# Second expert stage: ring slots by rows of the weights, a size for 32 tokens, loops for large sizes, and nested size tests

## The reference

```python
def moe_ffn(h, router_w, router_b, w1, b1, w2, b2):        # xt: 256 x 1024
    logits = (xt @ router_w + router_b)
    top_v, top_e = lax.top_k(logits, 4)
    gate = jax.nn.softmax(top_v, axis=-1)
    ...
        hb = xb @ w1[e] + b1[e]                            # xb: the tokens of expert e
        g, u = hb[:, :1024], hb[:, 1024:]
        g = jnp.minimum(g, 7.0)
        u = jnp.clip(u, -7.0, 7.0)
        glu = g * jax.nn.sigmoid(g * 1.702)
        return ((u + 1.0) * glu) @ w2[e] + b2[e]           # times its gate, added to the token
```

## Time and profile before

| | us |
|---|---|
| median of 3 runs | 2518.3 (2500.11 to 2536.43) |
| profiled execution | 2512.87 |
| its span, first to last instruction | 2511.1 |
| busy: PE, its weight loads, DVE, ACT | 2247.6, 1328.1, 589.5, 370.2 |
| mean granted clock of PE | 0.916 |
| read from HBM | 616.55 MB |

### The profile page before, as it was taken

How to read it: one execution, slowest core, us unless ns; L and a number is a source line. 1 busy time by engine, 2 the same in 40 slices (tenths; PEclk the granted TensorE clock), 3 DMA queues, 4 the chain that set the end, 5 groups by cost and what they waited for, 6 DMA issues and landing times.

```text
span 2511.1 us, 32392 instructions
## 1 busy us (share of the span) xinstructions
PE 2247.6 (90%) x12228; PEld 1328.1 (53%) x12229; DVE 589.5 (23%) x1216; ACT 370.2 (15%) x718; POOL 6.5 (0%) x23
## 2 busy tenths in 40 slices
PE   7969877889998997788858999899999999999996
PEld 5655445556545686633335554445455555555553
DVE  2352512211222015500031212111221222222113
ACT  1032101121111014300011111101011111111111
POOL 1000000000000000000000000000000000000000
PEclk9989997999999976588877989999998999999998
DMA  8822253998966340022225999859799999999990
GB/s 289 317 101 82 86 201 120 327 356 312 325 224 233 102 150 19 1 100 100 100 78 198 393 363 345 312 202 380 270 386 381 339 393 376 393 383 393 384 370 18
DMA packets 272763, 621.67 MB, mean 248 GB/s; under 512 B 12200, under 2 KB 19026, under 8 KB 272510
## 3 DMA queue, kind: packets, MB, share of 16 engines
q1 hardware_dynamic: 272302, 616.95, 67.1%
q10 hardware_dynamic: 208, 0.67, 0.1%
HBM read 616.55 MB, written 1.05 MB: 246 GB/s over the span
## 4 chain that ended last, share of the span: by engine, by line
PE 87%; DVE 6%; issue 4%; ACT 3%; POOL 0%; ACTq 0%; DVEq 0%; POOLq 0%
PE pair L1616 26%; PE pair L1410 16%; PE pair L1652 10%; PE pair L1671 8%; PE pair L1397 6%; PE pair L1689 4%; PE pair L1621 3%; PE pair L1655 2%; PE pair L1459 2%; PE pair L1451 1%; PE pair L1825 1%; PE pair L1434 1%; PE pair L1422 1%; PE pair L1702 1%; PE pair L1414 1%
## 5 line engine op out<-in xcount | busy, mean ns | idle before, releaser
L1616 PE MATMUL pair<-ring,r_at 128*64 128x256 f32 (+1 forms) x4864 | 662.0, 402 | 53.2 <-issue 49.5
L1616 PEld LDWEIGHTS pair<-ring,r_at 128*64 128x64 f32 (+1 forms) x4864 | 385.6, 143 | 317.2 <-issue 177.2
L1652 PE MATMUL pair<-ring,r_big 128*64 128x512 f32 x1152 | 263.9, 609 | 0.0
L1410 PE MATMUL pair<-ring,x_T 128*128 128x512 f32 (+1 forms) x608 | 236.9, 545 | 2.5 <-ACT r_big L719 1.1
L1671 PE MATMUL pair<-r_big,r_mix 128*128 128x64 f32 (+1 forms) x1600 | 204.3, 290 | 23.1 <-DVE r_big L1338 11.4
L1671 PEld LDWEIGHTS pair<-r_big,r_mix 128*128 128x128 f32 x1600 | 197.8, 205 | 34.0 <-issue 33.2
L1173 DVE TENSOR_SCALAR r_big<-iota,rank 128x128 f32<-128x128 f32 x100 | 24.1, 283 | 752.0 <-PE pair L1621 577.0
L1410 PEld LDWEIGHTS pair<-ring,x_T 128*128 128x128 f32 x608 | 107.5, 190 | 125.0 <-issue 123.0
L1652 PEld LDWEIGHTS pair<-ring,r_big 128*64 128x64 f32 x1152 | 80.4, 140 | 151.2 <-issue 149.9
L1397 PE MATMUL pair<-x_T,ring 128*128 128x256 f32 x656 | 152.8, 391 | 7.8 <-DVEq L838 6.4
L1397 PEld LDWEIGHTS pair<-x_T,ring 128*128 128x128 f32 x656 | 125.9, 195 | 32.3 <-issue 8.0
(11 more groups left out here) (310 smaller groups left out, 1602.7 us busy)
## 6 DMA issues: line engine op xcount, KB each, us to landing
ring<-exp_w SPq DMA_DIRECT2D x192, 2048.0 KB, 12.5
ring<-w_in SPq DMA_DIRECT2D x24, 2048.0 KB, 9.2
ring<-w_gate SPq DMA_DIRECT2D x16, 2048.0 KB, 11.4
ring<-w_up SPq DMA_DIRECT2D x16, 2048.0 KB, 13.4
ring<-w_down SPq DMA_DIRECT2D x16, 2048.0 KB, 9.2
ring<-mod_w SPq DMA_DIRECT2D x12, 2048.0 KB, 13.5
ring<-w_out SPq DMA_DIRECT2D x4, 2048.0 KB, 8.0
ring<-w_branch SPq DMA_DIRECT2D x3, 2048.0 KB, 7.6
```

The costliest lines, as they stand in the source:

```text
L1410: ins = mm(out[:, t, 0:n], xT[:, k, P * t:P * t + P], w[:, k, c0:c0 + n], start=(k == 0), stop=(k == nk - 1 and bias is None))
L1616: ins = mm(out, stat(k), w_[:, k, c0:c0 + n], start=(k == 0), stop=(bias is None and k == KD - 1))
L1652: ins = mm(ps[2][H2 * h:H2 * h + H2, 0:512], hT[:, at:at + H2], cols, start=beg, stop=end)
```

## The change

The gate and up weights of an expert are loaded in four slots of 256 whole rows (2048 columns) in place of four of 1024 rows x 512 columns. The six slots stay. Sizes become four: up to 32, 64, 128, and more. The tests are nested, `If` and `Else`, the smallest size first, once for all of an expert's up slots and once for its down slots, with the slots' waits inside. For up to 32 tokens the stationary operand has 32 columns, and gate and up, two halves each, go to four column groups; for up to 64, two column groups. Up to 128: loops on PE (`nc.Fori`) over the four column blocks for slots 1 to 3, each slot closed by a drain. More than 128: loops over everything, both halves of the tokens at once. The picks repeat every 32 or 64 slots (`slots_of`), so that gather and scatter are always 128 wide and have no size test. The hidden layer is limited, multiplied and transposed in one piece instead of two halves. The wait for `outputs_added` leaves `add_outputs` for its callers. Item `kvc` ahead of the stage is split in two, which aligns the stage's first slot with the ring.

```diff
 def size_of(eng, e):
-    return eng.value_load(sizes[0:1, bass.ds(e + 1, 1)], min_val=0, max_val=2)
+    return eng.value_load(sizes[0:1, bass.ds(e + 1, 1)], min_val=0, max_val=3)
+def smallest_first(eng, size, body):
+    with eng.If(size == 0):
+        body(H4)
+    with eng.Else():
+        with eng.If(size == 1):
+            body(H2)
+        with eng.Else():
+            with eng.If(size == 2):
+                body(P)
+            with eng.Else():
+                body(T)
...
-def expert2(slot, kind, e, half, wait):
+def expert2(slot, part, e, wait):
     sp.wait_ge(PD, wait)
-    if kind < 2:
-        src = w1e[bass.ds(e * D, D), 1024 * kind + 512 * half:1024 * kind + 512 * half + 512]
-        nk = KD
+    if part < 4:
+        src, nk = w1e[bass.ds(e * D + 2 * P * part, 2 * P), :], 2
     else:
-        src = w2e[bass.ds(e * D + 512 * half, 512), :]
-        nk = 4
+        src, nk = w2e[bass.ds(e * D + 512 * (part - 4), 512), :], 4
...
 # ACT, per expert
-    for half in range(2):
-        act.wait_ge(sem("gate_limited"), 2 * e + (1 + half))
...
-        s.activation(SG[:, 0:4 * w], GS[:, 0:4 * w], ACT.Sigmoid, scale=1.702)\
-    turned(2, 0, e, w)
-    by_size(act, size_next, rows_of(2, e + 1))
-    turned(2, 1, e, w)
+        act.wait_ge(sem("gate_limited"), e + 1)
+        ins = s.activation(SG[0:rows, 0:n], GS[0:rows, 0:n], ACT.Sigmoid, scale=1.702)
+    ins.then_inc(sem("sig_ready"), 1)
+    rows_of(2, e + 1)(P)
+    hidden_T2(e, w)
     outputs_and_picks(2, e, w, 6 * e + (base_pd2 + 6))
...
 # DVE, per expert
+    slots = iota if b == 1 else slots_of[:, bass.ds(size_of(dve, e) * P, P)]
...
+    dve.wait_ge(PD, 6 * e + (base_pd2 + 4))
+    v.tensor_scalar(gate, g_in, 7.0, None, ALU.min).then_inc(sem("gate_limited"), 1)
+    ins = v.tensor_scalar(up, u_in, 7.0, -7.0, ALU.min, ALU.max)
+    ins.then_inc(up_free, 1)
+    v.scalar_tensor_tensor(out=up, in0=up, scalar=1.0, in1=gate, op0=ALU.add, op1=ALU.mult)\
+    v.tensor_tensor(out=out, in0=up, in1=sig, op=ALU.mult).then_inc(sem("hidden_ready2"), 1)
...
 # PE
+def up_parts(w):
+    x32, x64, x128 = [lambda k, n=n: XG[:, k, 0:n] for n in (H4, H2, P)]
+    if w == H4:
+        return [(ps[0][H4 * q:H4 * q + H4, 0:512], x32, q, H4) for q in range(4)]
...
+def up_slot(w, j, n, i, e, buf):
+    pe.wait_ge(slot_loaded[(j + n) % RING], value_of(j + n, i, 6))
...
+    if w == P and n == 0:
+        pe.wait_ge(sem("pickT_ready2"), e + 1)
+    if w == P and n:
+        pe.sem_inc(sem("wide_rows_begun"), 1)
+        with nc.Fori(0, 4, engines=[pe.engine]) as q:
+            for k in range(2 * n, 2 * n + 2):
+                mm(pairs[:, bass.ds(q * 512, 512)], XG[:, k],
+                   ring[:, bass.ds(q * 512 + (j + n) % RING * SLOT + 2048 * (k % 2), 512)],
+                   start=(k == 0), stop=False)
+        if n < 3:
+            ins = pe.drain()
+    else:
+        for k in range(2 * n, 2 * n + 2):
+            for out, stat, q, rows in up_parts(w):
+                ins = mm(out, stat(k), w_[:, k % 2, 512 * q:512 * q + 512], start=(k == 0), stop=False)
+    if n == 3:
+        for out, stat, q, rows in up_parts(w):
+            ins = mm(out, ones[32 * q:32 * q + 1, 0:rows], b1q[32 * q:32 * q + 1, buf], start=False, stop=True)
+    ins.then_inc(PD, 1)
...
+def down(j, i, size, e):
+    def body(w):
+        turn_hidden2(w, e)
+        pe.wait_ge(sem("outputs_added2"), e + 2)
+        pe.wait_ge(sem("hiddenT_ready2"), e + 1)
+        for half in range(2):
+            down_slot(w, j, half, i)
+    smallest_first(pe, size, body)
...
+def expert2(i, par, j, e, size):
+    pe.wait_ge(sem(f"b1_loaded{buf}"), 16 * (PASS // 2) * i + 16 * (par // 2) + 16)
+    pe.wait_ge(sem("xg_ready2"), e + 1)
+    up(j, i, size, e, buf)
+    scatter2(e)
+    gather2(e + 1, 1 - buf)
+    pe.wait_ge(sem("hidden_ready2"), e + 1)
+    down(j + 4, i, size, e)
+    pe.wait_ge(sem("xg_ready2"), e + 2)
+    turn_picks2(buf)
```

More of the change, by code:

```diff
@@ new lines, in outputs_of_all @@
+            def outputs_of_all(e):
+                dve.wait_ge(PD, 6 * e + (base_pd2 + 6))
+                for t in range(NT):
+                    for h in range(2):
+                        v.scalar_tensor_tensor(out=ACC[:, t, 512 * h:512 * h + 512], in0=ps[2 + t][:, 512 * h:512 * h + 512],
+                                               scalar=comb0[:, t, bass.ds(e + 1, 1)],
+                                               in1=ACC[:, t, 512 * h:512 * h + 512], op0=ALU.mult, op1=ALU.add)
+                v.memset(YS, 0.0).then_inc(sem("ys_ready2"), 1)
@@ L1613, in body @@
                                  for t in range(NT)]
                     for k in range(KD):
-                        for out, stat, c0, n, rows in parts:
-                            ins = mm(out, stat(k), w_[:, k, c0:c0 + n], start=(k == 0),
-                                     stop=(bias is None and k == KD - 1))
-                    if bias is not None:
-                        q, buf = bias
-                        for out, stat, c0, n, rows in parts:
-                            ins = mm(out, ones[32 * q:32 * q + 1, 0:rows], b1q[32 * q:32 * q + 1, buf, c0:c0 + n],
-                                     start=False, stop=True)
+                        for out, stat, c0, n in parts:
+                            ins = mm(out, stat(k), w_[:, k, c0:c0 + n], start=(k == 0), stop=(k == KD - 1))
@@ L1637, in turn_hidden, with half_down @@
                 by_size(pe, size, body)
-            def half_down(j, load_value, hT, size, first, last):
+            def half_down(j, load_value, size):
                 pe.wait_ge(slot_loaded[j % RING], load_value)
@@ L1645, in body @@
                     for f in range(4):
-                        beg, end = first and f == 0, last and f == 3
+                        beg, end = f == 0, f == 3
                         for h in range(2):
@@ new lines, in down_of_all @@
+            def down_of_all():
+                with nc.Fori(0, 2, engines=[pe.engine]) as o_:
+                    for c in range(KD):
+                        for t in range(NT):
+                            mm(pairs[:, bass.ds(o_ * 512 + 2048 + 1024 * t, 512)],
+                               HTF[:, 1024 * t + P * c:1024 * t + P * c + P], W2_all[:, bass.ds(o_ * 512 + D * c, 512)],
+                               start=(c == 0), stop=(c == KD - 1))
+                pe.drain().then_inc(PD, 2)
```

337 lines of the change are left out of this document (216 added, 121 removed).

## The result

The changed kernel takes 2487.8 us, the median of 8 runs (2478.8 to 2492.9), beside 2516.5 for the kernel before in the same comparison: a ratio of 0.9889, with a 95% interval of 0.985 to 0.9928. It is 1.1% faster, where 2.8% was forecast. The second expert stage takes 1118.5 us (1344.4 to 2462.9) where it took 1145.5, 27 less; the sum had 1062 for it, 83.5 less (70 with the 13 set aside for the clock).

What follows compares the result with a forecast made beforehand. PE bound the kernel, with the weight DMA close behind in the second expert stage. That stage was to fall from 1145.5 to 1062 us (-83); 2511 - 83 + 13 for the clock = 2441 span, 2448 us forecast, range 2395 to 2540.

Steps and rivals of the forecast that it cites:

- the 13 set aside for the clock: Second expert stage: 13 us added because PE's products run at a lower clock after waiting for weight slots.
- Up of size 0: Up products of experts with at most 32 tokens: four column groups at once, 115 ns a record, 8.5 us instead of 16.7.
- Rival 3: Groups of 32 columns don't run four at once; experts up to 32 tokens take 33.9 us: +182, 2630 us; chance 0.05.
- A size-0 expert on PE: PE's time for one expert of at most 32 tokens in the second stage: 22.2 us, against 30.6 before.
- The new wait for the hidden layer's copy: Before the down products, PE waits for ACT's copy of the turned hidden layer: 0.7 to 1.0 us.
- The loops: PE loops in wide experts, three slots of four turns: 0.3 us a slot taken.
- Rival 1: Loops in the four wide experts cost 1 to 3 us a turn: 2448 plus 48 to 144 us; chance 0.12.
- Rows of 8 KB: Up-weight transfers in whole rows: 417 GB/s instead of 385, so 30.4 us of DMA an expert instead of 32.1.
- rival 4: Longer up-weight rows bring nothing: 32.1 us for 30.4 over about 19 DMA-paced experts, +34, 2482 us; chance 0.13.
- rival 2: Long skips over unused size bodies miss, two per expert at 4.28 us plus slow clock: +200, 2648 us; chance 0.12.
- nearest is the skip, so nothing: PE's size tests: skipping about 78 products was priced at nothing, like today's skip of 27; bounds nothing and 4.28 us.
- less half an expert for a full ring at the start: Experts 17 to 30: the six-slot weight ring, full at the start, saves about half an expert, 410 us for 426.

Runs made afterwards that it cites:

- without the large body: The changed kernel without the body for more than 128 tokens in all size tests of the second stage: 2436.0 us, ratio 0.9688.
- padded version with short jumps: The changed kernel with size tests once per slot, large sizes tested first, and 128 never-run instructions ahead of the expert loop: 2436.8 us, ratio 0.9696.
- versions with 58 and 52 us of issue waits in all: The changed kernel with tests per slot and large sizes first (2442.3 us, 0.9726), and the changed kernel without the over-128-token body (2436.0 us, 0.9688).

## Why the prediction was wrong

The sign and most terms were right, the size was not: the profiled span came to 2486.7, against 2441 by the sum, 45.7 more. By stretches the measured times are over the forecast by 10.5, 24.8, 22.5 and -1.3; less the 13 set aside for the clock that is 43.5. The rest is a stage that began 3.8 us later (1344.4; in the runs that change only PE's code or the rows it began anywhere from 1332 to 1352, so that this is an effect of the change is not shown), an end 1.2 us shorter, and rounding.

**What held.**
- Up of size 0: 110 ns a record (115 taken, 107 to 222 the bounds); bias 1.06 (1.3); down 3.64 (3.7); scatter 3.70 where nothing was waited for; gather 3.7. Rival 3 falls.
- A size-0 expert on PE: 20.8 us, start to start, for the first one without the large body, which waits for nothing but the copy (22.2 by the sum). Wide experts 6, 8 and 11 took 61.6 to 61.8 (63.4), the 64-token experts of 5 to 16 31.4 to 34.2 in the padded version with short jumps (33.9).
- The new wait for the hidden layer's copy: 34.0 us in 28 experts, 1.2 each (0.7 to 1.0 taken).
- The loops: 0.7 us a slot at most, 5.3 us in all (0.3 a slot taken). Rival 1 falls.
- The wait for both clamps in wide experts: 11.4 us in four, 2.8 each, as worked out.
- Rows of 8 KB: over 400 GB/s, 415 in several slices of the page's row (417 forecast), and 20 us when they are taken away, where rival 4 had priced 34. Rival 4 falls.
- The 32-token size: 2.6%, about 66 us. By the sum's own numbers, 22 x (33.9 - 30.4) = 77.

Slips in the arithmetic are small: the parts listed for the three sizes add up to 22.0, 33.6 and 63.2, not 22.2, 33.9 and 63.4, some 3 us over experts 5 to 16. In rival 2's full price, "5 x 22" has no source in the text: two skips at 4.28 lift a size-0 expert by 8.6, not by 22.

**The step that failed** is "nearest is the skip, so nothing", the price of the size tests. The row it leaned on was a jump over 27 products; the change made it 78, and the bounds were 0 and 4.28. What the runs showed: a jump in a bad place costs 3.1 to 4.2 us behind the up body and 2.4 to 3.7 behind the down body. Over the stage, back edges and loops included, it is 160.6 us of issue waits. That this was coming, the prediction's own sign said: gaps put down to issue ahead of scatter and picks of size 0 were to show rival 2. The sum had held 6 x 7 = 42 for back edges and 4 for the loops. Of the 115 left, most of what fell in experts 17 to 30 lay in time in which PE would have waited for weights; what fell in experts 0 to 16 made them 623.3 for the 588 forecast, 35 us. The versions with 58 and 52 us of issue waits in all, near the 46 of the sum, took 582 and 583 there, so the rest of that sum was good to about 1%.

The waits were rival 2's mechanism, and its gauge was fair: "it decides from about 2 us a skip". The 115 us over two skips in 32 experts are 1.8 us a skip. I gave it a chance only at its full price, 2648, and left out its mild form, between the forecast and the threshold, which is what came. The Trainium skill (Runtime: NRT & Kernel Launch, Instruction fetch mechanics) says that a taken branch to a target outside the current two-block window stalls; I had quoted it and gone by the one row instead. The trace agrees with it in kind: waits that follow the place of the code, move when 128 unused instructions are put ahead of it, and have a packet of instructions in them. What the runs give is a count: a jump of 42 products behind the up body cost 3.8 and 18.8 us before the scatter in two kernels, one of 54 cost 2.3, 7.1 and 16.6 in three, one of 78 cost 50.4, 51.0 and 31.5 in three layouts, one of 126 cost 92.0.

**The second mis-sized term** is experts 17 to 30: 410 by 14 x 30.4 = 426 less half an expert for a full ring at the start. No version shows that credit: 424 to 429 in the best. The ring is not full there: in the padded version with short jumps PE waits 2.6 us for weights in expert 17 itself and 4.8 in expert 18. The window of experts 18 to 30 in the padded version with short jumps, then in the changed kernel:

```profile
1948.00:2353.00 405.00, 313.09 (x1952) 126.60 (x1952) 77.22 (x130) 59.79 (x81) 0.00 (x0) 0.92 1.01 414
```

```profile
1997.00:2403.00 406.00, 310.74 (x1951) 132.96 (x1952) 77.21 (x130) 58.68 (x78) 0.00 (x0) 0.89 1.00 407
```

414 GB/s in 405 us against 407 in 406. So of the 22.5 us over the forecast about 16 are the credit and, by what is left, 6 the waits.

**The clock**, for which 13 us stood: the mean granted clock went from 0.916 to 0.888, and it costs where PE has just waited. Windows of the changed kernel, expert 2: the up body, the wait, the scatter behind it:

```profile
1401.50:1408.50 7.00, 7.00 (x68) 2.04 (x69) 0.48 (x2) 0.73 (x1) 0.00 (x0) 1.00 0.98 369
1409.60:1412.60 3.00, 0.00 (x0) 0.00 (x0) 2.74 (x4) 0.63 (x1) 0.00 (x0) 1.00 1.03 423
1412.70:1417.90 5.20, 5.20 (x9) 2.18 (x10) 0.00 (x0) 0.00 (x0) 0.00 (x0) 0.67 1.01 422
```

3 us without a matmul, and the next 5.2 us have a mean granted clock of 0.67, part at 2.4 and part at 1.2 GHz: 1.7 us more for the scatter. Behind the other waits of 3.1 to 3.5 us shown above the scatter took 5.37 to 6.71 us for 3.70, so the slow clock costs half to nine tenths of the wait again.

**What stays open**: which addresses make a jump miss. The places are shown to follow the layout; the rule behind them is not, nor how much time in a body hides a jump (before the picks all of it, before the scatter 0.6 us), nor what part of the waits before up is for weights. Neither is it shown why the loops in the wide down slots made the kernel slower by 0.7%.

## What to carry to other kernels

A body for a size that never comes is not free: it stands between the others, and each jump over it may cost 3 to 4 us, half to nine tenths as much again for the slow clock behind it, and all of it where that engine sets the pace. Keep the jumps short on both sides of the body that runs most: tests per part of the work, and a loop where it takes much code away (the large up body in one was worth 2.1%; the short down slots in one lost 0.7%). To see what an idle stretch waits for, count the packets of the instruction queue in it, and measure with some dead code put ahead before reading a difference below 1% as an effect of an edit. A saving on one engine is worth only what the next bound leaves: the same edit of the rows was worth 0.8% behind the faster PE and nothing before it.

## What the runs showed of the hardware

- A jump over 312 instructions stalled PE for 3.1 to 4.2 us at two places of a loop (13 of 13) and once in 9 at the other two; 128 unused instructions ahead of the loop changed which. One over 128 instructions stalled it for 2.5 to 3.1 us in 21 of 22, and never with the 128 ahead.
- In each of 28 such stalls of more than 3 us, in two kernels, the instruction queue moved one packet of 16 KB.
- A longer body ahead of the jump hides some of these stalls: behind up, 3.4 us behind 8 us of work and 2.8 behind 15; behind down, 3.2 in seven experts behind 3.6 us of work and none behind 7.1.
- Four groups of 32 columns take 110 ns per record of 512 columns; 64 records in 7.07 us.
- Ahead of a short loop on PE with register-addressed operands (four turns) stood a wait of 0.6 to 0.7 us, once per loop and not per turn; with tests around each slot it was 1.4 to 1.8.
